# Keys and values of a page in one transfer, two page splits and a gate split reordered, in a two-layer hybrid decoder step

## What is computed

```python
hist = nsa_pool[page_table].reshape(b, past, N_NSA_ROWS, C_KV, HEAD_DIM)
new_rows = jnp.stack([p['k_cmp'], p['v_cmp'], p['k_slc'], p['v_slc']], axis=2)
rows = jnp.concatenate([hist, new_rows], axis=1)
kc, vc, c_end = compress(rows[:, :, 0], rows[:, :, 1], pe_k, pe_v, wk1, wk2, wv1, wv2)
ks_blk = to_select_blocks(rows[:, :, 2])
vs_blk = to_select_blocks(rows[:, :, 3])
o_cmp, o_slc = nsa_core(p['q_c'], pos, kc, vc, c_end, ks_blk, vs_blk, ov)
...
# in nsa_core
imp = jnp.einsum('bqgrn,nm->bqgm', p_cmp, ov)
...
_, sel = lax.top_k(imp, min(SLC_TOP, n_slc))
```

## Time and profile before

| | us |
|---|---|
| median of three runs | 919.99 (919.67 to 920.89) |
| the profiled execution | 919.65 |
| its span in the trace | 918.0 |
| PE busy | 898.1 (98%) |
| PE weight loads busy | 836.8 (91%) |
| DVE, ACT, POOL busy | 648.2, 453.9, 193.8 |

### The profile page before, as it was taken

How to read it: one execution, slowest core, us unless ns; L and a number is a source line. 1 busy time by engine, 2 the same in 40 slices (tenths; PEclk the granted TensorE clock), 3 DMA queues, 4 the chain that set the end, 5 groups by cost and what they waited for, 6 DMA issues and landing times.

```text
span 918.0 us, 21372 instructions
## 1 busy us (share of the span) xinstructions
PE 898.1 (98%) x7904; PEld 836.8 (91%) x7904; DVE 648.2 (71%) x1449; ACT 453.9 (49%) x900; POOL 193.8 (21%) x321
## 2 busy tenths in 40 slices
PE   6999999999999999999999999999999999999997
PEld 6999998888888799999999998898888978999996
DVE  6999766677666467656769996676866565765664
ACT  6444665465443444334543447664654444443352
POOL 1200000347658300000000000013575771000000
PEclk9999999999999999999999999999999999999999
DMA  9762995735979873333675577765569799335321
GB/s 330 296 221 101 404 373 207 295 149 181 315 225 291 267 329 141 138 139 124 255 255 201 201 310 268 307 269 232 201 181 298 241 272 357 127 147 202 157 93 51
DMA packets 66359, 209.96 MB, mean 229 GB/s; under 512 B 12192, under 2 KB 49776, under 8 KB 56272
## 3 DMA queue, kind: packets, MB, share of 16 engines
q1 hardware_dynamic: 57200, 187.67, 55.9%
q0 software_dynamic: 8912, 20.92, 7.1%
q10 hardware_dynamic: 144, 0.01, 0.0%
HBM read 202.58 MB, written 41.36 MB: 266 GB/s over the span
## 4 chain that ended last, share of the span: by engine, by line
PE 89%; DVE 3%; ACT 2%; issue 2%; SPq 2%; DMA 1%; DVEq 0%; ACTq 0%
PE bank L1050 65%; PE bank L1310 8%; PE bank L1063 4%; SPq L874 2%; PE bank L1188 1%; PE bank L1180 1%; PE bank L1344 1%; PE bank L1217 1%; PE bank L1230 1%; PE bank L1441 1%; PE bank L1243 1%; ACT paged_r L1576 1%; DMA big<-in_w_tok 1%; PE bank L1412 1%; ACT kvp L1544 0%
## 5 line engine op out<-in xcount | busy, mean ns | idle before, releaser
L1822 DVE TENSOR_TENSOR big_r<-big,paged_r 128x1024 fp32r<-128x1024 f32 (+1 forms) x160 | 194.7, 1221 | 72.9 <-ACT paged_r L1576 72.0
L1050 PE MATMUL bank<-xnT_high_r,paged_r 128*128 128x288 f32 x768 | 231.7, 302 | 0.0
L1050 PE MATMUL bank<-xnT_r,paged_r 128*128 128x288 f32 x704 | 207.7, 295 | 0.0
L1050 PE MATMUL bank<-xnT_high_r,big_r 128*128 128x288 f32 x704 | 207.1, 294 | 0.0
L1576 ACT ACTIVATE paged_r<-big 128x1024 fp32r<-128x1024 f32 (+1 forms) x160 | 166.8, 1049 | 5.4 <-DMA big<-in_w_feat 2.7
L1050 PE MATMUL bank<-short_r,big_r 128*128 128x288 f32 x568 | 167.5, 295 | 0.0
L1050 PEld LDWEIGHTS bank<-xnT_high_r,paged_r 128*128 128x128 f32 x768 | 144.0, 187 | 4.4 <-issue 2.0
L1050 PEld LDWEIGHTS bank<-xnT_high_r,big_r 128*128 128x128 f32 x704 | 132.5, 188 | 0.0
L1050 PE MATMUL bank<-short_r,paged_r 128*128 128x288 f32 x440 | 131.2, 298 | 1.2 <-DVE big_r L1822 1.0
L1050 PEld LDWEIGHTS bank<-xnT_r,paged_r 128*128 128x128 f32 x704 | 132.3, 188 | 0.0
L1050 PE MATMUL bank<-kvp_r,paged_r 128*128 128x288 f32 x440 | 130.4, 296 | 0.0
(11 more groups left out here) (352 smaller groups left out, 1804.6 us busy)
## 6 DMA issues: line engine op xcount, KB each, us to landing
big<-in_w_tok SPq DMA_DIRECT2D x13, 2048.0 KB, 9.7
big<-in_w_feat SPq DMA_DIRECT2D x12, 2048.0 KB, 8.5
big<-in_w_gate SPq DMA_DIRECT2D x10, 2048.0 KB, 8.6
out_kept_dil<-in_cache_dil SPq DMA_DIRECT2D x16, 1020.0 KB, 13.0
paged<-in_pool SPq DMA_DIRECT2D x218, 64.0 KB, 4.3
big<-in_w_up SPq DMA_DIRECT2D x12, 1024.0 KB, 8.7
paged<-in_pool POOLq DMA_DIRECT2D x166, 64.0 KB, 4.6
big<-in_kv_win SPq DMA_DIRECT2D x4, 2048.0 KB, 9.0
```

The source lines that it names most:

```text
L1050: last = mm(out, l, r, start=(c == 0 and i == 0), stop=(c == n - 1 and i == 2))
L1822: v.tensor_tensor(l_part[:, rest], full[:, rest], h_part[:, rest].bitcast(FP32), ALU.subtract)\
```

## The change

1. A page's key and value (of cmp, or of slc) come in one transfer of 128 KB. A page key is now (kind, hb, request), eight transfers each; POOL takes 4 of the 8, of the first pair 2 of 8.
2. Places: a half tile holds one request. cmp of requests 0 and 1 goes to paged[1], of 2 and 3 to paged[0], of 4 and 5 to big[0], of 6 and 7 to paged[0]. slc goes to big[2], paged[1], `long` with x, and big[0]. kA of hb 1 goes to big[2], vA of hb 1 to paged[1], the first gate's weights to paged[0].
3. The waits of `load_pages` and of the loads follow from that, and the order of loads puts gate 1 ahead of the first two up weights.
4. For the pairs (0,1,1) and (1,0,1) `htail` stands ahead of the `psplit` of the piece two further on. The attention steps that stood between `hid` and `hpost` of two pieces now stand behind the whole piece, or ahead of the next.
5. Round and split of the first gate's first quarter stand behind `imp 1` and ahead of `impsum 1`.

```diff
-POOL_PAGES = 15
-POOL_PAGES_FIRST = 8
+POOL_PAGES = 4
+POOL_PAGES_FIRST = 2
...
         z = next(done)
         ends = z[3] and z[0:3] != (1, 1, 1)
-        return [("hid",) + z, *between] + [("hpost",) + z[0:3]] * ends + begin() + [("htail",) + z[0:3]] * ends
+        hpost, htail, ahead = [("hpost",) + z[0:3]] * ends, [("htail",) + z[0:3]] * ends, begin()
+        if z[0:3] in ((0, 1, 1), (1, 0, 1)):
+            return [("hid",) + z, *between] + hpost + ahead[0:1] + htail + ahead[1:]
+        return [("hid",) + z, *between] + hpost + ahead + htail
...
-           [("sgateA", 0), ("sscore", 1, "d4")] + piece(("cmpt", 0), ("sscore", 1, "mix"), ("sturn", 0, "win")) + \
-           [("sexp", 1, "A")] + piece() + \
+           [("sgateA", 0), ("sscore", 1, "d4")] + piece() + \
+           [("cmpt", 0), ("sscore", 1, "mix"), ("sturn", 0, "win"), ("sexp", 1, "A")] + piece() + \
...
-           [("impsum", 0), ("spv", 1, "mix"), ("sturn", 1, "anew")] + \
-           piece(("spv", 1, "anew"), ("soA", 1)) + piece() + [("kc", 1)] + \
+           [("impsum", 0), ("spv", 1, "mix"), ("sturn", 1, "anew")] + piece() + \
+           [("spv", 1, "anew"), ("soA", 1)] + piece() + [("kc", 1)] + \
...
-            ("imp", 1), ("spv", 0, "cnew"), ("sturn", 0, "slc1"), ("vc", 1), ("impsum", 1)] + splits(("gate", 0, 0), 0) + \
+            ("imp", 1)] + splits(("gate", 0, 0), 0) + [("spv", 0, "cnew"), ("sturn", 0, "slc1"), ("vc", 1), ("impsum", 1)] + \
...
+    big_slot = {("kA", 1): 2, ("vA", 1): 3}
...
-    loads = big_keys[0:-3] + [("kA", 1), ("vA", 1), ("win", 1), gate_keys[0]] + up_keys[0:2] + gate_keys[1:2]
+    loads = big_keys[0:-3] + [("kA", 1), ("vA", 1), ("win", 1)] + gate_keys[0:2] + up_keys[0:2]
...
+    pair_of = lambda kind, hb, bp: [(kind, hb, RB // 2 * bp + i) for i in range(RB // 2)]
+    page_keys = sum([pair_of(kind, hb, bp) for kind in ("cmp", "slc") for hb in range(HB) for bp in range(2)], [])
+    PAGE_HALVES = [(paged[1], 0), (paged[1], 1), (paged[0], 0), (paged[0], 1), (big[0], 0), (big[0], 1), (big[2], 0), (big[2], 1),
+                   (long, 0), (x[:, :, :].rearrange("p k n -> p (k n)"), 0)]
...
+        queue.wait_ge(*{("cmp", 0, 0): big_used(layer, split_keys[-2]), ("cmp", 0, 1): big_used(layer, split_keys[-1]),
+                        ("cmp", 1, 0): big_used(layer, ("kA", 0)), ("cmp", 1, 1): pages_used(layer, ("cmp", 0, b)),
+                        ("slc", 0, 0): big_used(layer, ("kA", 1)), ("slc", 0, 1): big_used(layer, ("vA", 1)),
+                        ("slc", 1, 0): PJ.is_full(("hid", 1, 0, 1)), ("slc", 1, 1): pages_used(layer, ("cmp", 1, 0))}[kind, hb, bp])
         for i in page_share(key, z):
-            b, g = divmod(i, PAGES)
-            src = a["pool"][Now.layer, bass.ds(numbers[hb][i], 1), :, which + 2 * (kind == "slc"), :]
-            queue.dma_start(pgb(key)[:, b, g, :], src.rearrange("a p n -> (a p) n")).then_inc(*PG[z].fill(key))
+            k = 2 * (kind == "slc")
+            src = a["pool"][layer, bass.ds(numbers[hb][b, i], 1), :, k:k + 2, :]
+            queue.dma_start(pgb(key)[:, i, :, :], src.rearrange("a p k n -> (a p) k n")).then_inc(*PG[z].fill(key))
...
+                    at_key = {("vA", 0): pair_of("cmp", 0, 0) + pair_of("cmp", 0, 1), ("kA", 1): pair_of("cmp", 1, 0),
+                              ("win", 1): pair_of("cmp", 1, 1) + pair_of("slc", 0, 0),
+                              FIRST: pair_of("slc", 0, 1) + pair_of("slc", 1, 0) + pair_of("slc", 1, 1)}
...
+                    if key == ("vA", 1):
+                        sp.wait_ge(*pages_used(layer, ("cmp", 0, 0)))
+                    elif key == FIRST:
+                        sp.wait_ge(*pages_used(layer, ("cmp", 1, 2)))
+                    elif key in up_keys[0:2]:
+                        sp.wait_ge(*pages_used(layer, ("slc", 0, 0)))
...
                     for pg in PG:
-                        act.wait_ge(*pg.is_full(("cmp", kind, hb, bp)))
+                        for page_key in pair_of("cmp", hb, bp):
+                            act.wait_ge(*pg.is_full(page_key))
```

More of the change, by code:

```diff
@@ L627, in bigb @@
         if k == gate_keys[0]:
-            return (paged if big is plain else paged_r)[1][:, :]
+            return (paged if big is plain else paged_r)[0][:, :]
+        if k == ("vA", 1):
+            return paged[1][:, :]
         return big[ring_of(k).buf(k)][:, :]
@@ L634, in halves_of @@
     def halves_of(k):
-        return {(2, UW.buf(k, 0))} if k in up_keys else set() if k == gate_keys[0] else {(ring_of(k).buf(k, 0), h) for h in range(2)}
+        if k in up_keys:
+            return {(2, UW.buf(k, 0))}
+        return set() if k in (gate_keys[0], ("vA", 1)) else {(ring_of(k).buf(k, 0), h) for h in range(2)}
     def place_used_by(layer, k):
@@ L690, in page_parts @@
         hb, kind, bp, lh = piece
-        low = piece_rows(paged_r[PAGE_SLOTS[("cmp", kind, hb)]], piece)
+        low = piece_rows(CMP_PLACE[hb, bp][1], piece)
         high = page_high[PIECES.index(piece) % 2].rearrange("p (m n) -> p m n", m=16)
@@ L695, in piece_rows @@
     def piece_rows(z, piece):
-        _, _, bp, lh = piece
-        rows = z[:, 2048 * bp:2048 * (bp + 1)].rearrange("p (m n) -> p m n", m=16)
-        return rows[:, :, 64 * lh:64 * (lh + 1)]
+        _, kind, _, lh = piece
+        rows = z[:, :].rearrange("p (m k n) -> p m k n", m=16, k=2)
+        return rows[:, :, kind, 64 * lh:64 * (lh + 1)]
     def piece_high(piece):
@@ L820, in pages_used @@
     def pages_used(layer, key):
-        kind, which, hb, h = key
+        kind, hb, b = key
         if kind == "cmp":
-            return PJ.is_full(("hid", hb, which, h), layer)
-        return O.is_full(("o", "s", hb), layer) if which else SC.is_full(("sscore", hb, "slc1"), layer)
+            return PJ.is_full(("hid", hb, 1, b // 2), layer)
+        return O.is_full(("o", "s", hb), layer)
     SROWS = {"d4": (("A",), [(P * c, P) for c in range(4)]),
@@ L964, in _ @@
                     if key == FIRST:
-                        sp.dma_start(dst[:, 0:2048], src[:, 0:2048]).then_inc(first_half_in[0], 16)
+                        for h in range(2):
+                            half = slice(2048 * h, 2048 * (h + 1))
+                            sp.dma_start(dst[:, half], src[:, half]).then_inc(first_half_in[h], 16)
                     else:
@@ L1367, in _ @@
                         for pg in PG:
-                            for h in range(2):
-                                pe.wait_ge(*pg.is_full(("slc", 0, hb, h)))
+                            for b in range(RB):
+                                pe.wait_ge(*pg.is_full(("slc", hb, b)))
                         for b in range(RB):
                             last = mm(bank[32 * b:32 * (b + 1), :].rearrange("p (g n) -> p g n", g=4),
-                                      q(3, b), pgb(("slc", 0, hb))[:, b, 4 * z:4 * z + 4, :], start=True, stop=True)
+                                      q(3, b), pgb(("slc", hb, b))[:, 4 * z:4 * z + 4, 0, :], start=True, stop=True)
                     last.then_inc(*SC.fill(s))
@@ L1435, in _ @@
                         z = int(what[-1])
-                        for pg in PG:
-                            for h in range(2):
-                                pe.wait_ge(*pg.is_full(("slc", 1, hb, h)))
                         for c in range(4):
@@ L1442, in _ @@
                                           pt[:, P * c + 32 * b:P * c + 32 * (b + 1)],
-                                          pgb(("slc", 1, hb))[:, b, 4 * z + c, :], start=False,
+                                          pgb(("slc", hb, b))[:, 4 * z + c, 1, :], start=False,
                                           stop=(z == 1 and c == 3), skip_group_check=True)
```

66 lines of the change are left out of this document (25 added, 41 removed).

## The result

The changed kernel takes 950.83 us (median of 6 runs, 947.2 to 954.2) against 920.18 of the kernel before, measured beside it: a ratio of 1.0328, with a 95% interval of 1.0315 to 1.0342. It is slower, as forecast, but by 30.7 us and not by 8, and 950.8 lies outside the range of 922.5 to 934.5. The profiled execution took 950.88 us, with a span of 949.2.

What follows compares the result with a forecast made beforehand. TensorE, busy 898.1 of 918.0 us, was taken as the bound. Terms summed to +4.0 us in layer 0 and +4.3 in layer 1, +8.3 together, giving 928.0 us, range 922.5 to 934.5.

Steps and rivals of the forecast that it cites:

- The late place of piece 2's pages: Sample stage: pages held until 226.9 us, rounding 4.95 us later, TensorE's transposes wait 4.9 us a layer; bounds 2.85 to 6.25.
- The nearest is the middle one: Landing of POOL's last page: 4.6 us row chosen among 2.8, 4.6, 5.9, plus 0.3 for twice the bytes; there at 237.05.
- check by rate: Sixteen 128 KB pages at 404 or 283 GB/s from about 229 us land at 234.2 to 236.4, without the vA load.
- formula of the Trainium skill for the SWDGE path: About 2.0 us plus bytes at 436 GB/s: last POOL page there at 234.45, delay 2.35 us instead of 4.9.
- kA: Load for requests 4 to 7 waits for spv mix, late for sscore d4: 0.6 us a layer, bounds 0.4 and 1.1.
- Pages of requests 6 and 7: Pages into paged0 wait for piece 7, delaying spv d4: 0.2 us, between 0 and 0.6.
- transfers pile up: Rival: page issues exceed the DMA rate; delay 6.25, kA 1.1, pages of 6 and 7 0.6, gate +1.2: 935.8 us, chance 0.14.
- first rival: It isn't slower: pages there by 232.1 us or delay not reaching TensorE; 918.5 us, without kA wait 916.9; chance 0.11.
- The two orders: htail ahead of psplit ends waits ahead of vc 0 (0.3) and kc 1 (0.8): gain 1.1 us a layer.
- First gate: Weights issued after piece 15, split ahead of the choice ends the 0.4 us wait: gain 0.3, bounds -0.4 and +1.2.

Runs made afterwards that it cites:

- e1_hold_va: Changed kernel, but SP issues the vA load of requests 0 to 3 only once the pages of requests 2 and 3 have landed: 944.9 us, 1.0265.
- e2_pair0_twice: Changed kernel, but key pieces of requests 2 and 3 are made from value pages of requests 0 and 1, all transfers kept: 927.59 us, 1.0072.
- e6_busy_pe: Changed kernel with 64 matmuls of unread result on TensorE in each layer's first long wait: 946.39 us, 1.026.
- e10_hold_busy: Changed kernel with the vA load held until pages of requests 2 and 3 landed, and 32 unread matmuls in each layer's first wait: 938.68 us, 1.0196.
- e7_hold_both: Changed kernel with the vA load held back, and SP's first slc pages held until cmp pages of requests 6 and 7 landed: 943.21 us, 1.0241.
- e3_before_htail: Kernel before, with only htail put ahead of the page split for two pairs and attention steps beside them reordered: 919.53 us, 0.999.

## Why the prediction missed the size

*The late place of piece 2's pages.* Right in its whole mechanism: the hold in `load_pages`, the issue (232.15 forecast for the last POOL page, 232.43 measured), ScalarE's round as the link, no slack at the transposes, the same in both layers. The step that failed is the landing: "The nearest is the middle one (SP's pages beside, the vA load coming 0.8 us earlier behind SP's pages), with 0.3 us for twice the bytes: 232.15 + 4.9". The row chosen had no large load beside it, the row of 5.9 us had one, and the second was the nearer; but it, too, was for 64 KB. It measured 9.9, and e1_hold_va gives 5.7 when the load is away. So the sum had 4.9 us a layer, and 9.8 and 9.2 were added; of the 4.9 and 4.3 us between, 4.3 and 4.1 go with the load (10.0 less 5.7, 9.4 less 5.3). In the trace's packet records a POOL page consists of 32 packets of 4096 bytes (16 in a page of 64 KB) and the vA load of 128 packets of 14336 bytes at 0.55 us (median). Of POOL's packets 24 to 44 a microsecond end between 231 and 235 us, before those of the load, and 12 to 20 from 235 to 240 us, while both are moved; in e1_hold_va it is 58 to 73 from 235 to 238 us. This is what was missing from "0.3 us for twice the bytes": twice the bytes are twice as many turns, each beside a packet three and a half times as large. The prediction's check by rate had left the load out, as it says ("without the vA load"). With its 1.8 MB the same working gives an estimate of 238.7 us at 404 GB/s and 242.9 at 283 (3.9 MB from 229 us on), around the 242.29 measured.

The Trainium skill (DMA: Bandwidth & Descriptors, section Queues, rings and completion order) says that each DMA engine takes turns between its queue rows packet by packet. e1_hold_va and the packet records agree with it; that the turns alone explain the 9.9 us was not shown, only that it goes with the load and what SP issues behind it. The 2.3 us that the formula of the Trainium skill for the SWDGE path gave in the prediction have 5.7 and 9.9 against them.

*The clock.* Not in the sum at all; a wait was priced at its own length and nothing behind it. It is 6.0 us of busy time in the changed kernel, 3.5 of it behind the first waits (e2_pair0_twice). e6_busy_pe and e10_hold_busy, which change only what TensorE does while it waits, win 4.4 and 6.2 us, of which 1.8 and 5.5 are busy time.

*kA.* Forecast 0.6 in each layer, measured 0.8 and none. The load is issued at 264.91 and 728.67 us and used at 273.2 and 736.2: the 7.5 us between load and use that were worked out are there, and in layer 1 they were enough: the load landed in 7.0 us, sooner than the quickest of the rows (7.9), and in layer 0 in 8.2. A small term, right in layer 0.

*Pages of requests 6 and 7.* Forecast 0.2, measured 2.4 and 3.1. The failed step is again the landing: the sum had POOL's eighth page issued at 269.4, 4.7 us behind piece 7, and gave it 2.8 to 4.6 us. The 4.7 us were right (282.16 less 277.42); the landing took 6.1. From the end of piece 7 to the round it was 10.9 us (277.4 to 288.3), against 7.5 to 9.3 in the sum. Part of it is the slc pages behind on SP's queue (e7_hold_both). This, the first wait and the gate are what the rival "transfers pile up" had named, with 24.6 us of waits instead of its 15.8. (A slip in the first rival weighs nothing here: without the kA wait it gives 917.3 us; the 916.9 written there leaves out the 0.2 us of requests 6 and 7 as well.)

*The two orders.* The waits for hidden values ended, 1.1 us a layer as worked out. e3_before_htail shows that in the kernel before most of it is given back: 0.6 us was gained where 2.2 was expected, because the next wait, for pages, was late by just that. In the changed kernel these pages are there.

*First gate.* Forecast a gain of 0.3, with +1.2 as the bound; measured +1.0 and +0.8. The 6.6 us that this half took among pages was the right row, 7.5 (median of the two halves) was measured. On the kernel before, this order wins 1.1 us more on the same chip (919.53 to 918.38), where 0.6 was expected; the intervals of the two overlap.

*The sum.* Forecast +8.3, measured +30.7. Of the difference of 22.4 us, 9.2 are the first wait, 6.0 the clock, 5.1 the pages of 6 and 7, 2.4 the gate; kA gives 0.4 back. That is 22.3.

The range was too narrow for a reason that could be read ahead: three terms depended on a landing among other transfers, and each had its bound from a row with less traffic than the changed kernel makes there. They were treated as three risks, but it is one.

## What to carry to other kernels

When a change moves a small transfer behind a late event, ask which large load is issued within the same microseconds, and take the landing from a row in which both are in flight; without such a row, the bound has to reach to the landing time of the large load itself. When a new wait is to come on TensorE, add what the clock can take afterwards (in these runs it fell behind every wait of 2.7 us or more in the sample stage, and behind five of the seven of 2.3 to 2.6), and look whether useful work can be put into the wait. And keep parts of a change apart: here two reorderings are worth 1.7 to 2.0 us, and the placement that came with them costs more than 30.

## What the runs showed of the hardware

- A 128 KB page issued 1 us behind a 1.8 MB load on another queue landed in 9.9 us; with the load and the pages behind it held back, in 5.7 us.
- After waits of 10.0 and of 5.7 us TensorE's clock was 0.50 and stayed so into the work behind them: 28 and 21 matmuls in 4 us, 47 and 53 in the same windows with the clock kept at 1.00. A wait of 3.1 us was followed by the low level as well (20 matmuls in 4 us), one of 2.4 us in the same kernel was not.
- 128 matmuls of no use, in the wait, made the kernel 4.4 us faster; 64 of them, with the load held, 6.2 us.
- Two pages that SP issued at 292.4 and 292.6 us of two kernels landed in 8.8 and 4.4 us: 128 KB among transfers of 128 KB, 64 KB among transfers of 64 KB.
